# Reordering the opening stage of a hybrid Hyena, state-space and expert-retrieval layer

## Time and profile before

| | us |
|---|---|
| median of 3 runs | 3739.07 (3738.95 to 3742.75) |
| the profiled execution, its own time | 3744.36 |
| span of its trace | 3742.6 |
| TensorE matmul busy | 3262.7 (87%) |
| VectorE busy | 1564.5 (42%) |
| GpSimd busy | 889.0 (24%) |
| ScalarE busy | 482.7 (13%) |
| DMA, mean over the span | 261 GB/s |

### The profile page before, as it was taken

The page is one execution under the profiler, slowest core; times in us unless marked ns, Lnnn a source line. Parts: engine busy times, 40 slices in busy tenths (PEclk is TensorE's granted clock), DMA queues, the critical chain, the costliest instruction groups (busy, mean ns, idle before and its releaser), DMA issues. The chain is left out here.

```text
span 3742.6 us, 32912 instructions
## 1 busy us (share of the span) xinstructions
PE 3262.7 (87%) x11164; PEld 2002.2 (53%) x11164; DVE 1564.5 (42%) x2876; ACT 482.7 (13%) x964; POOL 889.0 (24%) x619
## 2 busy tenths in 40 slices
PE   6999999999999998999899997867677776677766
PEld 2466758576675857777788843433233333333322
DVE  6544444343443533111000014156656556565565
ACT  2212212122121212000000000010110101101010
POOL 0010202111020211101000000065545554455553
PEclk8999999999999999999999998988888888888888
DMA  9654454545545364343444452289999999999997
GB/s 361 258 222 174 180 202 148 225 151 199 189 166 212 132 230 163 141 174 112 146 149 145 157 216 101 101 368 426 426 427 426 426 427 426 426 426 427 427 426 311
DMA packets 151603, 977.60 MB, mean 261 GB/s; under 512 B 17640, under 2 KB 30345, under 8 KB 44297
## 3 DMA queue, kind: packets, MB, share of 16 engines
q0 software_dynamic: 73728, 536.90, 34.1%
q1 hardware_dynamic: 65962, 416.86, 30.2%
q10 hardware_dynamic: 11872, 23.30, 1.7%
HBM read 955.80 MB, written 21.20 MB: 261 GB/s over the span
## 5 line engine op out<-in xcount | busy, mean ns | idle before, releaser
L1004 PE MATMUL ps<-mT,ring 128*128 128x256 f32 (+1 forms) x4096 | 1171.0, 446 | 3.0 <-PEq L215 3.0
L1004 PEld LDWEIGHTS ps<-mT,ring 128*128 128x128 f32 x4096 | 774.9, 190 | 392.8 <-issue 323.2
L1945 PE MATMUL ps<-mT,diagonal 128*128 128x512 f32 x1024 | 484.0, 634 | 344.3 <-ACT diagonal L1755 340.0
L1945 PEld LDWEIGHTS ps<-mT,diagonal 128*128 128x128 f32 x1024 | 205.8, 204 | 622.6 <-issue 622.6
L1857 DVE CUSTOM_DVE_ANT_0 ring<-ring,h_rows 128x2048 f32<-128x2048 f32 x128 | 293.6, 2293 | 468.6 <-DMA ring<-in_peer_u_dram,expert_index 465.1
L1945 PE MATMUL ps<-v_rows,diagonal 128*128 128x512 f32 x1024 | 445.0, 592 | 1.3 <-DMA v_rows<-in_peer_v_dram,expert_index 1.3
L1945 PEld LDWEIGHTS ps<-v_rows,diagonal 128*128 128x128 f32 x1024 | 194.4, 190 | 246.8 <-issue 246.8
L1857 DVE CUSTOM_DVE_ANT_0 u_rows<-u_rows,h_rows 128x2048 f32<-128x2048 f32 x128 | 289.6, 2290 | 12.4 <-DMA u_rows<-in_peer_u_dram,expert_index 11.5
L1710 POOL DMA_INDIRECT ring<-in_peer_u_dram,expert_index x128 | 125.1, 977 | 703.9 <-issue 703.9
L673 POOL TENSOR_TENSOR dd<-mask_f,dt_g 128x1024 f32<-128x1024 f32 x16 | 30.4, 1898 | 952.1 <-DVE dt_g L915 951.4
L1710 POOL DMA_INDIRECT v_rows<-in_peer_v_dram,expert_index x128 | 206.2, 1611 | 203.6 <-PE ps L1945 163.7
(11 more groups left out here) (316 smaller groups left out, 2539.8 us busy)
## 6 DMA issues: line engine op xcount, KB each, us to landing
ring<-in_w_stream_dram SPq DMA_DIRECT2D x160, 1024.0 KB, 4.8
ada_tiles<-in_w_ada_dram SPq DMA_DIRECT2D x64, 1024.0 KB, 6.7
ring<-in_w_mix_dram SPq DMA_DIRECT2D x64, 768.0 KB, 4.3
ring<-in_w_mod_dram SPq DMA_DIRECT2D x32, 1024.0 KB, 11.4
rows<-cum_rows_scratch SPq DMA_DIRECT2D x16, 1536.0 KB, 12.9
ring<-in_w_out_dram SPq DMA_DIRECT2D x16, 1024.0 KB, 4.8
ring<-in_w_q_dram SPq DMA_DIRECT2D x16, 1024.0 KB, 4.8
hf_c<-hf_scratch SPq DMA_DIRECT2D x8, 1024.0 KB, 7.4
```

The source lines that it names most:

```text
L1004: mm = nc.tensor.matmul(ps[:, k % 4, 0:n], m.ring[:, slot, kt * P:(kt + 1) * P], m.mT[:, kt, 0:n], start=(kt == 0), stop=(kt == KT - 1))
L1945: mm = nc.tensor.matmul(ps[:, 4 * t + b, :], dia[:, n, :], v_slot[n][:, b * 512:(b + 1) * 512], start=False, stop=False)
```

## The change

- Filter slices run one step ahead: slices 0 and 1 before the loop; in step s TensorE does `filter_rows(s+1)` and `sum_absolutes(s)` ahead of `ada_products(s)`, and `transform(s-1)` at the end of the step instead of `transform(s-2)`. VectorE and ScalarE follow: `windowed(s+1)`, `normalise_filter(s)`, `absolute(s+1)`, `copy_spectrum(s-2)`.
- `turn_ada` writes into the modulation chunk's own bank (ADA), so `ada_products(s)` waits for `modulation(s-1)`. Bank MISC is left to the step projection, which goes over the steps: two tiles in each of steps 3 to 7, six behind them. Its weights come in three parts after the ring tiles of steps 2, 4 and 6.
- The context rows are rescaled on GpSimd in front of its work of step 2.
- The three small loads (bias, skip, selector) go ahead of the ring's first tiles.
- Each spectrum is stored once, three parts with one transfer; `block_c` reads it with three transfers, the two small ones making the fourth part.

```diff
...
         piece_in = [sem(f"filter_piece_{n}_loaded") for n in range(NCHUNK)]
-        wdt_loaded = sem("wdt_loaded")
+        wdt_loaded = [sem(f"wdt_part_{n}_loaded") for n in range(3)]
+        x_sd = sem("ctx_deviations_ready")
...
         def bank_of(k):
-    return F0 + k % 2 if k < LATE else (F0, F0 + 1, ADA, F0)[k - LATE]
+    return F0 + k % 2 if k < LATE else (F0, F0 + 1, ABS, F0)[k - LATE]
...
         sp.dma_start(dst[:], src).then_inc(first, 16)
+    for dst, src in ((m.adab, d.adab), (skip, d.hy_skip), (sel2, d.sel2)):
+        sp.dma_start(dst[:], src).then_inc(small, 16)
...
     sp.dma_start(xin[:, 0:TT, :], d.x).then_inc(x_loaded[0], 16)
-    for dst, src in ((m.adab, d.adab), (skip, d.hy_skip), (sel2, d.sel2)):
-        sp.dma_start(dst[:], src).then_inc(small, 16)
...
             sp.dma_start(m.ring[:, b, :], d.w_mod[RING * s + b]).then_inc(m.w_full[b], 16)
-        if s % 2 and s < SLOTS - 1:
+        if s % 2 == 0:
+            sp.dma_start(wdt[:, 5 * (s // 2 - 1):5 * (s // 2 - 1) + 5 + (s == 6), :],
+                         d.w_dt[:, 5 * (s // 2 - 1):5 * (s // 2 - 1) + 5 + (s == 6), :]).then_inc(wdt_loaded[s // 2 - 1], 16)
+        elif s < SLOTS - 1:
             filter_piece((s + 1) // 2)
-    sp.dma_start(wdt[:], d.w_dt).then_inc(wdt_loaded, 16)
...
     for s in range(SLOTS):
+        if s == 2:
+            pool.wait_ge(x_sd, 1)
+            for t in range(TT, 2 * TT):
+                nc.gpsimd.tensor_scalar(xin[:, t, :], xin[:, t, :], mv[:, t, 0:1], x_rstd[:, t:t + 1],
+                                        ALU.subtract, ALU.mult).then_inc(x_normed, 1)
...
         if s:
-            act.wait_ge(f_stored, 48 * s)
+            act.wait_ge(f_stored, 16 * s)
...
         act.wait_ge(f_out, s + 1)
-        spec = d.hf[s]
-        act.dma_start(spec[:, 0:3 * CH], hf[:].rearrange("p a b -> p (a b)")).then_inc(f_stored, 16)
-        act.dma_start(spec[0:HALF, 3 * CH:4 * CH], hf[HALF:P, 2, :]).then_inc(f_stored, 16)
-        act.dma_start(spec[HALF:P, 3 * CH:4 * CH], hf[0:HALF, 2, :]).then_inc(f_stored, 16)
+        act.dma_start(d.hf[s], hf[:].rearrange("p a b -> p (a b)")).then_inc(f_stored, 16)
...
         nc.scalar.activation(dst[:], harg[0:(64, P)[n], :], ACT.Sin).then_inc(ff_sin, 1)
-    for s in range(SLOTS):
-        if s >= 3:
-            copy_spectrum(s - 3)
-        if s == 0:
-            copy_ada(s)
-        absolute(s)
-        if s < 2:
-            act.wait_ge(x_varied, s + 1)
-            of = slice(TT * s, TT * s + TT)
-            nc.scalar.activation(x_rstd[:, of], x_var[:, of], ACT.Sqrt).then_inc(x_std, 1)
-        if s:
-            copy_ada(s)
+    def x_deviation(n):
+        act.wait_ge(x_varied, n + 1)
+        of = slice(TT * n, TT * n + TT)
+        nc.scalar.activation(x_rstd[:, of], x_var[:, of], ACT.Sqrt).then_inc(x_std, 1)
+
+    copy_ada(0)
+    absolute(0)
+    x_deviation(0)
+    absolute(1)
+    x_deviation(1)
+    for s in range(1, SLOTS):
+        if s >= 2:
+            copy_spectrum(s - 2)
+        if s < SLOTS - 1:
+            absolute(s + 1)
+        copy_ada(s)
...
             modulate(k)
-    copy_spectrum(SLOTS - 3)
+    copy_spectrum(SLOTS - 2)
     modulate(LATE + 1)
-    copy_spectrum(SLOTS - 2)
+    copy_spectrum(SLOTS - 1)
     modulate(LATE + 3)
-    copy_spectrum(SLOTS - 1)
-    act.wait_ge(f_stored, 48 * SLOTS)
+    act.wait_ge(f_stored, 16 * SLOTS)
...
         newton_rsqrt(nc, v, c, x_rstd[:, of], x_var[:, of], x_tmp[:, of])
+        if n:
+            v.sem_inc(x_sd, 1)
+            return
...
         v.wait_ge(ada_pe, s + 1)
-        cols = ps[:, MISC, 8 * s:8 * s + 8].rearrange("p (a b) -> p a b", b=2)
+        cols = ps[:, ADA, 0:8].rearrange("p (a b) -> p a b", b=2)
...
     v.wait_ge(small, 48)
-    for s in range(SLOTS):
-        if s % 2 == 0:
-            v.wait_ge(piece_in[s // 2], 48)
-        windowed(s)
-        if s:
-            modulation(s - 1)
-        if s < 2:
-            normalise_x(s)
-        if s:
-            normalise_filter(s - 1)
+    v.wait_ge(piece_in[0], 48)
+    windowed(0)
+    windowed(1)
+    normalise_x(0)
+    normalise_filter(0)
+    for s in range(1, SLOTS):
+        modulation(s - 1)
+        if s < SLOTS - 1:
+            if s % 2:
+                v.wait_ge(piece_in[(s + 1) // 2], 48)
+            windowed(s + 1)
+        if s == 1:
+            normalise_x(1)
+        normalise_filter(s)
...
         modulate(k)
-    normalise_filter(SLOTS - 1)
...
         pe.wait_ge(ada_a, s + 1)
-        if s:
-            pe.wait_ge(mod_c, s)
         for j in range(4):
-            mm = nc.tensor.matmul(ps[:, MISC, 8 * s + 2 * j:8 * s + 2 * j + 2], ada_rows[:, j * P:(j + 1) * P], sel2[:],
+            mm = nc.tensor.matmul(ps[:, ADA, 2 * j:2 * j + 2], ada_rows[:, j * P:(j + 1) * P], sel2[:],
...
             pe.wait_ge(f_win, TT * s)
-        if s >= 3:
-            pe.wait_ge(mod_a, 4 * (s - 2))
+        if s >= 4:
+            pe.wait_ge(mod_a, 4 * (s - 3))
...
         if s:
-            pe.wait_ge(ada_a, s)
+            pe.wait_ge(mod_c, s)
...
         for k in tiles:
+            if k % 5 == 0 and k < 15:
+                pe.wait_ge(wdt_loaded[k // 5], 16)
...
     pe.wait_ge(consts, 5)
-    for s in range(SLOTS):
-        if s == 0:
-            ada_products(s)
-            pe.wait_ge(ff_sin, 2)
-            filter_rows(s)
-            pe.wait_ge(small, 48)
-        else:
-            sum_absolutes(s - 1)
-            turn_ada(s - 1)
-            filter_rows(s)
-            ada_products(s)
+    ada_products(0)
+    pe.wait_ge(ff_sin, 2)
+    filter_rows(0)
+    pe.wait_ge(small, 48)
+    filter_rows(1)
+    sum_absolutes(0)
+    for s in range(1, SLOTS):
+        turn_ada(s - 1)
+        if s < SLOTS - 1:
+            filter_rows(s + 1)
+        if s >= 2:
+            sum_absolutes(s)
+        ada_products(s)
+        if s == 1:
+            sum_absolutes(s)
+            pe.wait_ge(dft_in, 16)
...
             pe.wait_ge(x_normed, 2 * TT)
-            pe.wait_ge(dft_in, 16)
+        if s >= 3:
+            pe.wait_ge(mod_a, 4 * (s - 2))
...
-            pe.wait_ge(f_win, TT * s + TT)
+            pe.wait_ge(f_win, TT * min(s + 2, SLOTS))
             transpose(k)
-        if s >= 2:
-            transform(s - 2)
+        if s >= 3:
+            project_dt(tiles_of(s - 1))
+        transform(s - 1)
     turn_ada(SLOTS - 1)
-    sum_absolutes(SLOTS - 1)
     pe.wait_ge(mod_a, 2 * LATE)
+    pe.wait_ge(f_eps, SLOTS)
...
         transpose(k)
-    transform(SLOTS - 2)
+    project_dt(tiles_of(SLOTS - 1))
+    transform(SLOTS - 1)
...
     transpose(LATE + 3)
-    pe.wait_ge(wdt_loaded, 16)
-    pe.wait_ge(mod_c, SLOTS)
-    project_dt(range(LATE))
-    transform(SLOTS - 1)
     pe.wait_ge(mod_v, 4)
+    pe.wait_ge(mod_a, 2 * LATE + 2)
+    project_dt(range(LATE, LATE + 3))
     pe.wait_ge(mod_a, 2 * LATE + 4)
-    project_dt(range(LATE, KT))
+    project_dt(range(LATE + 3, KT))
...
+    def load_hf(n, o):
+        sp.dma_start(hf[:, o, 0:3, :].rearrange("p a b -> p (a b)"), d.hf[n]).then_inc(hf_in[o], 16)
+        sp.dma_start(hf[0:HALF, o, 3, :], d.hf[n, HALF:P, 2 * CH:3 * CH]).then_inc(hf_in[o], 16)
+        sp.dma_start(hf[HALF:P, o, 3, :], d.hf[n, 0:HALF, 2 * CH:3 * CH]).then_inc(hf_in[o], 16)
+
...
     for o in range(ORDER):
-        sp.dma_start(hf[:, o].rearrange("p a b -> p (a b)"), d.hf[o]).then_inc(hf_in[o], 16)
+        load_hf(o, o)
...
                 sp.wait_ge(mul, 6 * c + 3)
-                sp.dma_start(hf[:, 0].rearrange("p a b -> p (a b)"), d.hf[ORDER * c + ORDER]).then_inc(hf_in[0], 16)
+                load_hf(ORDER * c + ORDER, 0)
...
                 sp.wait_ge(mul, 6 * c + 6)
-                sp.dma_start(hf[:, 1].rearrange("p a b -> p (a b)"), d.hf[ORDER * c + ORDER + 1]).then_inc(hf_in[1], 16)
+                load_hf(ORDER * c + (ORDER + 1), 1)
...
             v.wait_ge(dft, 2 * c + o + 1)
-            v.wait_ge(hf_in[o], 16 * c + 16)
+            v.wait_ge(hf_in[o], 48 * c + 48)
...
 SCRATCH = {
-    "hf": (ORDER * NCHUNK, P, 4 * CH),
+    "hf": (ORDER * NCHUNK, P, 3 * CH),
...
     "y_ssd": (GROUPS, P, XTILES * T),
```

## The result

| | before | changed |
|---|---|---|
| median, us | 3740.91 (4 runs, 3738.95 to 3743.70) | 3761.34 (4 runs, 3755.39 to 3764.12) |
| profiled execution | 3744.36 (span 3742.6) | 3755.39 (span 3753.7) |
| N, first matmul of the next stage | 166.2 | 184.1 |

A forecast was written before the change was run, and what follows sets the result against it. The opening stage was taken as bound by its weight stream. Chunk 7 ending 27.1 us later, less 12.7 gained in the tail, gave 14.4 us slower: 3753.5 from a median of 3739.07, range 3747 to 3763.

The forecast's parts named there:

- GpSimd: Step 2: each of two context-row rescalings moved to GpSimd takes 3.3 us, against 1.3 on VectorE.
- The gate: Chunks 1, 3, 5 wait for a filter piece queued behind the chunk's own tiles, emptying the DMA queue 6.8 us each.
- The starts named as signs: Chunks 1, 3 and 5 start near 49, 91 and 129, each behind a wait for the filter piece.
- empty queue: After a piece lands: filter rows 2.0, summing 1.0, first tile 2.0, issue to first bytes 1.8, in all 6.8 us.
- the summing: Two TensorE passes between filter rows and the chunk's first tile, priced at 1.0 us at the lower clock.
- Step 1: Piece 1 lands at 47.1 and chunk 1 starts at 49.3, against 34.9 in the kernel before.
- 1.2 us of later start for the whole stream: Three small loads moved ahead of the ring on SP delay the stream by 1.2 us, bounds 0 and 1.8.
- From above the two-input 128x2048 takes 4.5: Upper bound for one GpSimd rescaling, taken from a two-input operation; the lower bound was 2.1 us.
- The rule on SBUF: Step 2: by the skill's rule the filter product waits for the second rescaling, chunk 2 about 1.3 us later still.
- Tail: From the end of chunk 7 to the next stage's first matmul: 12.7 us gained, with ten step projection tiles moved into the steps.
- Hyena stage: Three spectrum transfers instead of one and 16 more issues on SP cost 0, bounds 0 to 3 us.
- Rival (a): Gates at chunks 1, 3, 5 cost nothing, only the tail counts: 12.6 us faster, 3726.5; chance 0.16.

The follow-up runs named there:

- e2: Changed kernel with the filter pieces' loads issued earlier, ahead of the tiles they were queued behind: N 166.7, ratio to before 0.9998.
- e4: Kernel before with only three added waits, TensorE waiting for filter pieces 1, 2, 3 ahead of chunks 1, 3, 5: N 178.8, ratio 1.0036.
- e1: Changed kernel with the context rows rescaled on VectorE again: N 179.7, ratio to before 1.0030.
- e3: Changed kernel with both the filter pieces loaded early and the context rows rescaled on VectorE: N 162.0, ratio to before 0.9977.
- e5: Kernel before with only the step projection spread over the steps, modulation ahead of the window product: N 161.0, ratio 0.9988.
- e6: Kernel before with only the single store of each spectrum and the three loads in the Hyena stage: N 163.3, ratio 0.9983.
- e9: e8 with chunk rows 1 copied before the context deviation, filter 1 and columns 1 before context rows, step 2's spectrum before transposes: N 156.0, ratio to before 0.9978.
- e10: Kernel before with the spread step projection and the single spectrum store together: N 158.8, ratio 0.9983.
- e8: e3 with VectorE's first two modulation columns moved up: N 159.3, ratio to before 0.9975.
- e11: e10 with the three small loads ahead of the ring: N 159.3, ratio to before 0.9979.
- e7: e3 with three probe instructions on GpSimd, a fill and two subtract-and-multiply on an idle 128x2048 tile: N 168.5, single execution.

## Why the prediction was right

The forecast was 3753.5, 14.4 us slower; measured were 20 us (15 to 25), and in the profiled execution 17.9 in the stage, where the forecast had all of its 14.4. The sign, the place and the mechanism of the gates were right. One large price, GpSimd's, was wrong, and so were some small ones. The total is nearer than its terms, which is partly luck: 9.4 us priced too low stand against 5.9 priced too high.

- *The gate.* Predicted steps from chunk 2 to 3, 3 to 4, 4 to 5, 5 to 6 and 6 to 7: 23.7, 14.3, 23.8, 14.3, 12.4. Measured: 24.0, 14.5, 22.1, 13.5, 12.4. The starts named as signs, near 49, 91 and 129 for chunks 1, 3 and 5, came at 46.8, 97.7 and 134.2, the later ones shifted by chunk 2. Of the 6.8 us of empty queue behind each piece some 5, 7.5 and 4.5 were measured. The prediction put the summing at 1.0 "at the lower clock"; that is its time at the higher one. At the lower clock it takes 2.05 (in the kernel before at 48.9, in the changed one at 95.7). On the other side piece 3 landed 17.3 us after the first reload, not 19.7. e2 and e4 show that it is the wait and not the work: 17.4 us given back by moving three loads, 12.6 us lost by adding three waits.
- *Step 1.* Predicted start 49.3, measured 46.8. The term that failed is "1.2 us of later start for the whole stream". The first ring tile was indeed issued 1.2 us later (4.54 instead of 3.38), but piece 1 did not inherit it: it landed at 44.8, not at 47.1. Why piece 1 came even earlier than before stays open; its own issues were not held up as before (SP needed 4.4 us for the two halves there and 1.1 here), but no run singles this out.
- *GpSimd.* "From above the two-input 128x2048 takes 4.5" was no bound. A rescaling takes 7.2 instead of 3.3, 7.9 us more for the two. This is the term that was mis-sized. It moved chunk 2, but its price in N is less than 7.9, since the later steps take part of it back: without it N falls by 4.4 to 4.7 (e1, e3). The stage's miss of 3.5 us is made up so: GpSimd +7.9, the earlier step 1 -2.4, the summing behind GpSimd at the lower clock +1.0, steps 2 to 4 +0.5, steps 4 to 6 -2.5, the tail -1.0.
- *The rule on SBUF.* The Trainium skill (SBUF — State Buffer, "Who interferes with whom") would have had the filter product wait for GpSimd's whole instruction. In the changed kernel it started at 59.95, inside GpSimd's 55.84 to 63.09, and took 1.63 instead of 1.23: slowed, not held (the profile gives GpSimd's ends only roughly, but this one lies 1.5 us behind the product's). For this pair the measurement decides against the rule.
- *Tail.* From the end of chunk 7 (163.7) to N: 20.4 measured, 21.4 predicted, 34.1 before. The shorter tail is there; what the spread gives by itself is the 5.2 us of e5.
- *Hyena stage.* Predicted 0, measured 0 (e6: 334.4 us in both).
- *Rival (a)*, that the gate costs nothing, is what e2 and e3 make true by moving the loads: 162.0 in e3, though not the 153.6 that (a) implied. VectorE's and ScalarE's order then holds chunks 1 and 2, and without that e9 reaches 156.0.

The slower kernel thus holds two gains (7.4 us in e10) and two losses (gates 17.4 to 17.7, GpSimd 4.4 to 4.7). What is left, some 3 us, is the distance from e10 to e3 and belongs to the rest of the reordering. VectorE's columns behind its long work are a likely part of it (e8 and e9 give back 6.0), but no run takes this rest apart. The filters one step ahead gave nothing that the times show. By N e10, without them, is 3.2 us ahead of e3 and 0.5 ahead of e8; e9, with them, is 2.8 ahead of e10, but it moves VectorE's and ScalarE's order too. The fastest by N is e9, 10.2 us less than before; by time e3, e8, e9, e10 and e11 can't be told apart, all 0.2% faster than before.

## What to carry to other kernels

When an instruction is moved ahead of the one that frees a buffer ring, look at where its operand stands in the load queue: if it is queued behind that ring's own tiles, every such step drains the queue, and the price is the whole way from landing to the first new bytes. Move the load along with its user: here moving three loads gave back 17.4 us of N. Price work moved to another engine by a row of the same operation there, or leave the range open at the top; a row with more inputs is no upper bound.

## What the runs showed of the hardware

- On GpSimd a subtract-and-multiply of 128x2048 floats with one tensor input takes 7.15 to 7.47 us, more than the addition of two tensors of that size (4.53); VectorE does it in 1.3. A fill takes 1.80.
- While GpSimd runs such an instruction, some VectorE instructions stand still. In e7 a VectorE `tensor_scalar` of 64x256 with one SBUF input, 0.28 us otherwise, started 0.2 us behind GpSimd's first, took 7.07 and ended at 13.91, where GpSimd's ended at 13.77. A second one started at 19.51 beside GpSimd's second, took 1.97 instead of 0.28 and ended at 21.48, again 0.14 behind it. This agrees with the Trainium skill (SBUF — State Buffer, "Who interferes with whom"), by which a `tensor_scalar` can run in a mode that needs the port pair shared with GpSimd, and then can't start until the other engine lets go. Which mode these ran in the traces do not show.
- VectorE instructions with two SBUF inputs did both. Three `scalar_tensor_tensor` were held for part of GpSimd's second instruction (5.53 us instead of 1.3, ended 1.9 before it), and in the changed kernel the filter product lost only 0.4. But a `tensor_tensor` of 128x2 (L121, 0.16 otherwise) took 1.11 beside GpSimd's halves' sum of 33.92 to 35.21 and ended at 35.23. What decides between held and slowed was not tried.
- The two half-width spectrum loads and 16 more issues on SP in the Hyena stage cost nothing that its 334.4 us show.
